# Hybrid decoder trunk on one Trainium2 core: the query latent and half of the key latent projected in three fp32r passes over split raw tokens

## The chip, the cores and the metric

The kernel runs on one core of one Trainium2 chip. The metric is the device time of one execution in microseconds (us). Before the change the median of three runs is 1300.8 us (1300.68 to 1301.29).

## What is computed

One layer of a decoder trunk on 272 tokens (16 learned meta tokens and 256 real ones) of width 1024: a Mamba-2 branch and a latent-attention branch side by side, then a mixture of 32 experts.

```python
hn = rms_norm(h, norm_mix[i])
u = hn @ w_in[i]
z, xbc, dt_raw, q_a, kv_a, gate_logits = jnp.split(u, IN_SPLITS, axis=-1)
y_ssd = ssd_branch(z, xbc, dt_raw, ...) @ w_ssd_out[i]
y_mla = mla_branch(q_a, kv_a, ...) @ w_o[i]      # begins with rms_norm(q_a), rms_norm(c_kv)
h = h + (g_ssd * y_ssd + g_mla * y_mla) @ w_out[i]
h = h + moe_ffn(rms_norm(h, norm_ffn[i]), ...)
```

The change touches two slices of the product `hn @ w_in`: `q_a` (384 columns, the query latent) and the block of 320 columns that the kernel calls `dkv` (32 of `dt_raw`, 256 of the key latent, 32 of its rotary part). Both latents are normed over their own columns afterwards.

## The kernel before

Everything runs in one program with one instruction stream for each engine, in an order written out by hand, with semaphores between the streams. Each engine takes its instructions in that order. ACT is ScalarE, DVE is VectorE, PE is TensorE, SP issues the DMAs.

**The front.** SP issues at the start, in this order: the transposed tokens in two halves (`hnT`), between and behind them the `dkv` weights in two halves, then the tokens in rows (`xtok`, four DMAs), the `qa` weights (1.5 MB, inside the loop over `SLABS`), the small vectors `vec`, and further weight slabs. DVE multiplies `hnT` by the gains of the norm, but not yet by the norm itself (L1072). PE multiplies this raw `hnT` by `dkv` and then by `qa` in plain float32 (the loops at L1622 to L1637 and L1647 to L1654). The token norms `rsx` come later, out of `xtok` (squares on ACT L657 and DVE L1076, then twelve tiny DVE steps in `rstd`, L1041 to L1064), and are multiplied in when ACT reads the banks (L679 to L688, L697 to L699). `spread_norms` on PE, behind the first `qa` matmul, broadcasts the norms over the partitions; DVE then makes `hnN`, the normed tokens (L1083), and ACT and DVE split it into a rounded part `hn_hi` (fp32r, L666) and the rest `hn_lo` (L1087).

**The feature units.** All other columns of `w_in` are made by `split_mm`: for each 128 columns the weights are split as well, `hi_of(p)` on ACT (L673) and `lo_of(p)` on DVE (L1100), into one of three buffers `split[p % 3]`, and PE makes three fp32r passes, hi·hi, hi·lo and lo·hi, over 8 blocks k. The first eight units, `cv` 0 to 7, feed a causal convolution. For unit c ACT reads the bank twice (`conv_in`, L707 and L712), DVE does three steps (`conv_of`, L1137 and L1138), ACT the tanh (`tanh_of`, L719), DVE the last product (`silu_of`, L1146). `conv_in(c)` waits, from c = 2 on, for `conv_of(c - 2)`, and PE's unit u waits until the bank of unit u - 2 has been read. The order on ACT in this stretch is

```python
for c in range(4):
    conv_in(c)
    hi_of(c + 3)
    if c:
        tanh_of(c - 1)
```

and on DVE

```python
for c in range(4):
    if c < 3:
        lo_of(c + 3)
    conv_of(c)
    if c:
        silu_of(c - 1)
```

Ahead of that loop DVE has `lo_of(0)` and `lo_of(1)`, the norm of the key latent (`rstd(rsk, ...)`), the rotary steps of `ckk` (L1108 to L1120), `lo_of(2)`, and the norm of the query latent (`rstd(rsq, ...)`, behind `proj_read` 5, ACT's read of the last `qa` bank). Behind the front come attention, the scan, the output projections (to about 384 us), and then the 32 experts, whose weights (about 400 MB) stream in as buffers come free.

## Time and profile before

| | |
|---|---|
| median of three runs | 1300.8 us (1300.68 to 1301.29) |
| the profiled execution's own time | 1301.11 us |
| its span in the profile | 1299.1 us |
| PE busy in the span | 1271.6 us (98%) |
| DVE busy | 461.1 us (35%) |
| ACT busy | 348.6 us (27%) |
| DMA | 467.24 MB, 360 GB/s in the mean |

One execution of the program is taken by the profiler. Times are from the start of the span. Some 2 us of the device time lie around the span (1301.11 less 1299.1). "Busy" is the time in which at least one instruction of the engine ran; the ends of matmuls are modelled. The share of an engine over the whole span says little about a stretch: DVE's 35% is an average over a first part in which it is nearly always busy and an expert part in which it idles.

### The profile page before, as it was taken

How to read it: one execution, taken by the hardware profiler on the slowest of the kernel's cores; microseconds unless marked ns; L12 is line 12 of the kernel's file. 1: busy time of each engine (PE TensorE's matmuls, PEld its weight loads, DVE VectorE, ACT ScalarE, POOL GpSimd, SP SyncE). 2: the span in 40 equal slices, each digit the busy share in tenths (PEclk: the TensorE clock that was granted, in tenths of full speed). 3: DMA queues.
4: the chain of work that ended last, by engine and by line, in shares of the span. 5: the costliest groups of instructions: out<-in, count | busy, mean ns of one | idle time of the engine just before them, and what ended most of it. 6: DMA issues, size and time to landing. Idle time of an engine off the chain costs nothing.

```text
span 1299.1 us, 17685 instructions
## 1 busy us (share of the span) xinstructions
PE 1271.6 (98%) x7139; PEld 646.0 (50%) x7139; DVE 461.1 (35%) x1072; ACT 348.6 (27%) x671; POOL 28.7 (2%) x46
## 2 busy tenths in 40 slices
PE   9999999999999999999999999999999999999997
PEld 7889999999973333333333233333333333323332
DVE  5978889887652112111121111112111112111112
ACT  4667788654441011110110110011110011010102
POOL 1000000022010000000000000000000000000000
PEclk9999999999999999999999999999999999999999
DMA  8332255457889999999999999999999999999996
GB/s 309 128 142 120 97 230 221 170 195 287 318 315 426 420 408 427 429 429 428 430 433 430 430 427 431 431 435 430 431 430 427 431 434 432 430 431 433 424 427 284
DMA packets 32180, 467.24 MB, mean 360 GB/s; under 512 B 4112, under 2 KB 4144, under 8 KB 8704
## 3 DMA queue, kind: packets, MB, share of 16 engines
q1 hardware_dynamic: 31840, 466.00, 85.8%
q8 instruction: 36, 0.59, 0.2%
q10 hardware_dynamic: 288, 0.52, 0.1%
q14 instruction: 16, 0.13, 0.0%
HBM read 465.43 MB, written 1.08 MB: 359 GB/s over the span
## 4 chain that ended last, share of the span: by engine, by line
PE 46%; DMA 23%; DVE 0%; SPq 0%; issue 0%; ACT 0%; DVEq 0%
PE bank L1593 44%; DMA ring<-wts_dram 16%; DMA work<-wts_dram 7%; PE bank L1994 1%; PE bank L2000 1%; PE bank L2024 1%; SPq L433 0%; SPq L567 0%; DVE work L1587 0%; DVE work L1553 0%; ACT work L1004 0%; DVE work L1497 0%; DVE work L1569 0%; DVEq L107 0%; DVE work L1499 0%
## 5 line engine op out<-in xcount | busy, mean ns | idle before, releaser
L1593 PE MATMUL bank<-ring,work 128*64 128x512 f32 (+2 forms) x2168 | 490.0, 586 | 13.1 <-DMA ring<-wts_dram 12.8
L1593 PE MATMUL bank<-work 128*64 128x512 f32 (+8 forms) x2184 | 430.3, 550 | 6.3 <-DMA work<-wts_dram 4.3
L1593 PEld LDWEIGHTS bank<-ring,work 128*64 128x64 f32 (+1 forms) x2168 | 156.4, 138 | 297.3 <-issue 263.9
L1593 PEld LDWEIGHTS bank<-work 128*64 128x64 f32 (+3 forms) x2184 | 148.5, 143 | 258.9 <-issue 239.1
L1593 PE MATMUL bank<-hn_hi,split 128*128 128x256 f32 (+1 forms) x896 | 172.2, 287 | 0.3 <-ACT work L712 0.2
L1520 DVE COPY work<-bank 128x256 f32<-128x256 f32 x30 | 12.7, 425 | 447.3 <-PE bank L2024 447.3
L1593 PEld LDWEIGHTS bank<-hn_hi,split 128*128 128x128 f32 x896 | 141.3, 188 | 1.0 <-ACT work L712 0.4
L1593 PE MATMUL bank<-hn_lo,split 128*128 128x256 f32 (+1 forms) x448 | 127.1, 284 | 0.0
L1100 DVE TENSOR_TENSOR split<-ring,split 128x1024 fp32r<-128x1024 f32 x88 | 109.7, 1248 | 23.1 <-ACT split L673 22.7
L1497 DVE TENSOR_SCALAR work<-bank 128x512 f32<-128x512 f32 x32 | 22.2, 692 | 262.5 <-PE bank L1593 262.5
L931 ACT ACTIVATE work<-bank 128x512 f32<-128x512 f32 x31 | 18.5, 598 | 325.6 <-PE bank L1593 325.6
L673 ACT ACTIVATE split<-ring 128x1024 fp32r<-128x1024 f32 x88 | 92.5, 1055 | 23.5 <-PE bank L1593 23.4
L1593 PEld LDWEIGHTS bank<-hn_lo,split 128*128 128x128 f32 x448 | 84.4, 188 | 0.1
L952 ACT ACTIVATE work<-bank 128x512 f32<-128x512 f32 x30 | 17.9, 598 | 190.1 <-PE bank L1593 190.1
L946 ACT ACTIVATE work<-bank 128x512 f32<-128x512 f32 x32 | 19.1, 598 | 155.0 <-PE bank L2000 155.0
L935 ACT ACTIVATE work<-bank 128x512 f32<-128x512 f32 x31 | 18.5, 598 | 105.8 <-PE bank L1994 105.8
L1593 PE MATMUL bank<-y_hi,split 128*128 128x256 f32 x256 | 46.2, 283 | 0.0
L1593 PEld LDWEIGHTS bank<-y_hi,split 128*128 128x128 f32 x256 | 40.0, 192 | 0.0
L1593 PE MATMUL bank<-y_lo,split 128*128 128x256 f32 x128 | 36.2, 283 | 0.0
L1593 PE MATMUL bank<-attn_hi,split 128*128 128x256 f32 (+1 forms) x144 | 28.2, 290 | 0.0
L2000 PEld LDWEIGHTS bank<-shifted,work 128*128 128x128 f32 x128 | 13.4, 140 | 26.0 <-issue 26.0
L832 ACT ACTIVATE work<-ring,small 128x256 f32<-128x256 f32 x64 | 24.4, 453 | 5.7 <-PE bank L1593 5.2
(302 smaller groups left out, 939.6 us busy)
## 6 DMA issues: line engine op xcount, KB each, us to landing
ring<-wts_dram SPq DMA_DIRECT2D x83, 2048.0 KB, 19.1
ring<-wts_dram SPq DMA_DIRECT2D x20, 4096.0 KB, 30.3
work<-wts_dram SPq DMA_DIRECT2D x20, 4096.0 KB, 29.3
ring<-slabs_dram SPq DMA_DIRECT2D x23, 2048.0 KB, 8.6
work<-wts_dram SPq DMA_DIRECT2D x23, 2048.0 KB, 14.4
...
```

Source lines behind the costliest of these rows:

```text
L673: a.activation(split[p % NSPLIT][:, 0], piece(p), ACT.Copy).then_inc(hi_ready, 1)
L832: last = a.activation(decay[c % 2][:, j, at:at + SEQ - lo], spread[:, c % 3, j, lo:SEQ], ACT.Relu, scale=-1.0, bias=As[:, col:col + 1])
L931: a.activation(xg[:, :], bank[7][:, :], ACT.Copy).then_inc(xg_ready, 1)
L935: a.activation(xgT[:, :, :].rearrange("p j t -> p (j t)"), bank[7][:, :], ACT.Copy).then_inc(xgT_ready, 1)
L946: a.activation(actT[:, :, :].rearrange("p j t -> p (j t)"), bank[7][:, :], ACT.Copy, scale=0.5).then_inc(actT_ready, 1)
L952: a.activation(ob[:, :], bank[6][:, :], ACT.Copy).then_inc(ob_ready, 1)
L1100: d.tensor_tensor(split[p % NSPLIT][:, 1], piece(p), split[p % NSPLIT][:, 0], ALU.subtract).then_inc(lo_ready, 1)
L1497: d.tensor_scalar(glu[:, :], bank[4][:, :], LIMIT, None, ALU.min).then_inc(glu_ready, 1)
L1593: return pe.matmul(o, lhsT, rhs, start=start, stop=stop)
L1994: last = pe.transpose(bank[7][:, j * P:(j + 1) * P], xg[:, j * P:(j + 1) * P], ident[:, :])
L2000: last = pe.transpose(bank[7][:, j * P:(j + 1) * P], act[:, j * P:(j + 1) * P], ident[:, :])
L2024: last = pe.transpose(bank[to][:, b * P:(b + 1) * P], hotw[:, b, :, :].rearrange("p i s -> p (i s)"), ident[:, :])
```

## The change

The `qa` product and blocks k = 4 to 7 of the `dkv` product, for the two blocks of 128 tokens, are no longer made in float32. The raw tokens, the `qa` weights and the second half of the `dkv` weights are each split into an fp32r part and the rest: ACT makes `raw_hi`, `dkv_w_hi` and `qa_w_hi`, DVE `raw_lo`, `dkv_w_lo` and `qa_w_lo`, and PE takes three fp32r passes over them. The last 16 tokens (`tail_latents`) stay in float32 and go ahead of the second half of the others. The `qa` weights are loaded in two halves, the first ahead of `xtok`, the second and `vec` behind it. The norms of both latents are made in one chain (`rsqrt` over five columns) behind `proj_read` 5. `lo_of(2)` comes ahead of that chain and `lo_of(3)` behind it; in the loop over c, `lo_of(4)` and `lo_of(5)` stand ahead of `conv_of(0)` and `conv_of(1)`. The `vec` scalings go behind `lo_of(1)`, and `hi_of(2)` on ACT goes between the two reads of the `qa` banks. New buffers overlay memory that is free at that time. The semaphores `hn_hi_ready` and `hn_lo_ready` become `front_hi_ready` and `front_lo_ready`, which count the new splits too. Left out below: the overlays and views, the names of the semaphores, and the two places of the loop over `SLABS` from which `qa` and `vec` are taken.

```diff
--- before.py
+++ after.py
...
@@ -398,15 +406,19 @@
 
         @block.sync
         def _(sp):
-            half_T, half_dkv = KD // 2 * L, KD // 2 * DKV
+            half_T, half_dkv, half_qa = KD // 2 * L, KD // 2 * DKV, KD // 2 * QL
+            qa_dram = slabs[:, OFF[SLAB["qa"]]:OFF[SLAB["qa"]] + 2 * half_qa]
             sp.dma_start(w(3072 - KD, KD + half_T), xt[:, 0:KD + half_T]).then_inc(xT_in[0], 16)
             sp.dma_start(slab("dkv")[:, 0:half_dkv], slabs[:, 0:half_dkv]).then_inc(dkv_half_in, 16)
             sp.dma_start(w(3072 + half_T, half_T), xt[:, KD + half_T:KD + 2 * half_T]).then_inc(xT_in[1], 16)
             sp.dma_start(slab("dkv")[:, half_dkv:2 * half_dkv], slabs[:, half_dkv:2 * half_dkv]).then_inc(slab_in[0], 16)
+            sp.dma_start(slab("qa")[:, 0:half_qa], qa_dram[:, 0:half_qa]).then_inc(qa_half_in, 16)
             sp.dma_start(xtok[NMETA:P, 0, :], x[0:P - NMETA, :]).then_inc(x_in[0], 16)
             sp.dma_start(xtok[0:NMETA, 0, :], meta).then_inc(x_in[0], 16)
             sp.dma_start(xtok[:, 1, :], x[P - NMETA:2 * P - NMETA, :]).then_inc(x_in[1], 16)
             sp.dma_start(xtok[0:TAIL, 2, :], x[2 * P - NMETA:SEQ, :]).then_inc(x_in[1], 16)
+            sp.dma_start(slab("qa")[:, half_qa:2 * half_qa], qa_dram[:, half_qa:2 * half_qa]).then_inc(slab_in[1], 16)
+            sp.dma_start(vec[:, :], vecs).then_inc(vec_in, 16)
 
             def pair_of(e, h):
                 return wts[bass.ds((e * E_UNITS + 2 * h) * P, 2 * P), :].rearrange("(p i) c -> p i c", i=2)
...
@@ -651,6 +661,21 @@
         def _(a):
             a.wait_ge(consts_ready, 2)
             a.activation(spare, small[:, 15:16], ACT.Square)
+            qa_w = slab("qa").rearrange("p (k n) -> p k n", k=KD)
+
+            def qa_hi_of(h):
+                ks = slice(h * (KD // 2), (h + 1) * (KD // 2))
+                a.activation(qa_w_hi[:, ks, :], qa_w[:, ks, :], ACT.Copy).then_inc(front_hi_ready, 1)
+
+            for h in range(2):
+                ks = slice(h * (KD // 2), (h + 1) * (KD // 2))
+                a.wait_ge(hnT_ready, h + 2)
+                a.activation(raw_hi[:, ks, :], hnT[:, ks, :], ACT.Copy).then_inc(front_hi_ready, 1)
+            a.wait_ge(*arrived("dkv"))
+            a.activation(dkv_w_hi, slab("dkv").rearrange("p (k n) -> p k n", k=KD)[:, KD // 2:KD, :],
+                         ACT.Copy).then_inc(front_hi_ready, 1)
+            a.wait_ge(qa_half_in, 16)
+            qa_hi_of(0)
             for b in (0, 2):
                 n = BLOCKS[b][1]
                 a.wait_ge(x_in[b // 2], 32)
...
@@ -663,7 +688,7 @@
 
             def hn_hi_of(i):
                 a.wait_ge(hnN_ready, i + 1)
-                a.activation(hn_hi[:, 4 * i:4 * i + 4, :], hnN[:, 4 * i:4 * i + 4, :], ACT.Copy).then_inc(hn_hi_ready, 1)
+                a.activation(hn_hi[:, 4 * i:4 * i + 4, :], hnN[:, 4 * i:4 * i + 4, :], ACT.Copy).then_inc(front_hi_ready, 1)
 
             def hi_of(p):
 
@@ -672,6 +697,8 @@
                     a.wait_ge(*PIECES[p - NSPLIT][2])
                 a.activation(split[p % NSPLIT][:, 0], piece(p), ACT.Copy).then_inc(hi_ready, 1)
 
+            a.wait_ge(*arrived("qa"))
+            qa_hi_of(1)
             a.wait_ge(rsx_ready, 1)
             for b in range(2):
                 a.wait_ge(proj_done, b + 1)
@@ -688,10 +715,12 @@
             a.activation(mid[0:TAIL, 2, :], tail_mid, ACT.Copy, scale=rsx[0:TAIL, 2:3]).then_inc(proj_read, 1)
             for j in range(2):
                 hn_hi_of(j)
-            for p in range(NSPLIT):
+            for p in range(2):
                 hi_of(p)
             a.wait_ge(rsxq_ready, 1)
             for b in range(2):
+                if b:
+                    hi_of(2)
                 a.wait_ge(proj_done, b + 4)
                 ps = bank[3 + b]
                 a.activation(junk2[:, 768 + b * QL:768 + (b + 1) * QL], ps[:, 0:QL], ACT.Square,
...
@@ -1071,22 +1100,43 @@
                 ks = slice(h * (KD // 2), (h + 1) * (KD // 2))
                 d.tensor_tensor(hnT[:, ks, :], hnT[:, ks, :], norm_mix[:, ks].unsqueeze(2).to_broadcast([P, KD // 2, L]),
                                 ALU.mult).then_inc(hnT_ready, 1)
+            qa_w = slab("qa").rearrange("p (k n) -> p k n", k=KD)
+
+            def front_lo_of(n, lo, whole, hi, h):
+                ks = slice(h * (KD // 2), (h + 1) * (KD // 2))
+                d.wait_ge(front_hi_ready, n)
+                d.tensor_tensor(lo[:, ks, :], whole[:, ks, :], hi[:, ks, :], ALU.subtract).then_inc(front_lo_ready, 1)
+
+            d.wait_ge(hnT_ready, 3)
+            front_lo_of(1, raw_lo, hnT, raw_hi, 0)
+            front_lo_of(2, raw_lo, hnT, raw_hi, 1)
+            d.wait_ge(front_hi_ready, 3)
+            d.tensor_tensor(dkv_w_lo, slab("dkv").rearrange("p (k n) -> p k n", k=KD)[:, KD // 2:KD, :], dkv_w_hi,
+                            ALU.subtract).then_inc(front_lo_ready, 1)
+            front_lo_of(4, qa_w_lo, qa_w, qa_w_hi, 0)
             d.wait_ge(consts_ready, 2)
             d.wait_ge(x_in[1], 32)
             link(d.tensor_tensor_reduce(out=junk[:, 1, :], in0=xtok[:, 1, :], in1=xtok[:, 1, :], scale=1.0, scalar=0.0,
                                         op0=ALU.mult, op1=ALU.add, accum_out=ssx[:, 1:2]))
             d.wait_ge(x_squared, 2)
             rstd(rsx, ssx, D, EPS, rsx_ready)
+            front_lo_of(5, qa_w_lo, qa_w, qa_w_hi, 1)
             d.wait_ge(rsx_spread, 1)
             d.tensor_copy(rsxq[:, :], bank[7][:, 0:2]).then_inc(rsxq_ready, 1)
             for i in range(2):
                 d.tensor_tensor(hnN[:, 4 * i:4 * i + 4, :], hnT[:, 4 * i:4 * i + 4, :],
                                 bank[6][:, 0:L].unsqueeze(1).to_broadcast([P, 4, L]), ALU.mult).then_inc(hnN_ready, 1)
             for i in range(2):
-                d.wait_ge(hn_hi_ready, i + 1)
-                d.tensor_tensor(hn_lo[:, 4 * i:4 * i + 4, :], hnN[:, 4 * i:4 * i + 4, :], hn_hi[:, 4 * i:4 * i + 4, :],
-                                ALU.subtract).then_inc(hn_lo_ready, 1)
-
+                front_lo_of(6 + i, hn_lo, hnN, hn_hi, i)
+
+            def lo_of(p):
+
+                d.wait_ge(hi_ready, p + 1)
+                d.tensor_tensor(split[p % NSPLIT][:, 1], piece(p), split[p % NSPLIT][:, 0], ALU.subtract).then_inc(lo_ready, 1)
+
+
+            for p in range(2):
+                lo_of(p)
             d.wait_ge(vec_in, 16)
             w_router = v("w_router").rearrange("p (k e) -> p k e", k=KD)
             d.tensor_tensor(w_router, w_router, v("norm_ffn").unsqueeze(2).to_broadcast([P, KD, E]), ALU.mult).then_inc(vec_scaled, 1)
...
@@ -1094,16 +1144,14 @@
             d.tensor_scalar(v("conv_b"), v("conv_b"), 0.5, None, ALU.mult).then_inc(vec_scaled, 1)
             link(d.tensor_scalar(v("ssd_norm"), v("ssd_norm"), 0.5, None, ALU.mult))
 
-            def lo_of(p):
-
-                d.wait_ge(hi_ready, p + 1)
-                d.tensor_tensor(split[p % NSPLIT][:, 1], piece(p), split[p % NSPLIT][:, 0], ALU.subtract).then_inc(lo_ready, 1)
-
-
-            for p in range(2):
-                lo_of(p)
-            d.wait_ge(proj_read, 3)
-            rstd(rsk, ssk, KVL, MLA_EPS)
+            lo_of(2)
+            d.wait_ge(proj_read, 5)
+            d.tensor_scalar(ssk, ssk, 1.0 / KVL, MLA_EPS, ALU.mult, ALU.add)
+            link(d.tensor_scalar(ssq, ssq, 1.0 / QL, MLA_EPS, ALU.mult, ALU.add))
+            rsqrt(sm(11, 5), sm(3, 5), nrt)
+            for b in range(2):
+                d.tensor_scalar(qa[:, b, :], qa[:, b, :], rsq[:, b:b + 1], None, ALU.mult)
+            lo_of(3)
             for b in range(NB):
                 d.tensor_scalar(ckk[:, b, 0:KVL], mid[:, b, HEADS_S:HEADS_S + KVL], rsk[:, b:b + 1], None, ALU.mult)
             d.memset(ckk[:, :, KVL:KVL + ROPE], 0.0)
@@ -1117,17 +1165,12 @@
             link(d.tensor_tensor(kr[:, 3], k1, sinv, ALU.mult))
             for at in (KVL + ROPE, KVL + 2 * ROPE):
                 d.tensor_tensor(ckk[:, :, at:at + 16], kr[:, 0], kr[:, 1], ALU.subtract)
-                d.tensor_tensor(ckk[:, :, at + 16:at + ROPE], kr[:, 2], kr[:, 3], ALU.add)
+                last = d.tensor_tensor(ckk[:, :, at + 16:at + ROPE], kr[:, 2], kr[:, 3], ALU.add)
+            last.then_inc(latent_ready, 1)
 
             dt3 = dtv.rearrange("p (b h) -> p b h", b=NB)
             link(d.tensor_tensor(dt3, mid[:, :, 0:HEADS_S], v("dt_bias").unsqueeze(1).to_broadcast([P, NB, HEADS_S]), ALU.add))
             d.scalar_tensor_tensor(dta[:, :], dtv[:, :], -1.0, dtv[:, :], ALU.mult, ALU.max).then_inc(dt_abs, 1)
-            lo_of(2)
-            d.wait_ge(proj_read, 5)
-            rstd(rsq, ssq, QL, MLA_EPS)
-            for b in range(2):
-                last = d.tensor_scalar(qa[:, b, :], qa[:, b, :], rsq[:, b:b + 1], None, ALU.mult)
-            last.then_inc(latent_ready, 1)
 
             def conv_of(c):
 
...
@@ -1148,8 +1191,8 @@
 
             d.wait_ge(consts_ready, 4)
             for c in range(4):
-                if c < 3:
-                    lo_of(c + 3)
+                if c < 2:
+                    lo_of(c + 4)
                 conv_of(c)
                 if c:
                     silu_of(c - 1)
...
@@ -1619,23 +1662,31 @@
             pe.wait_ge(hnT_ready, 1)
             fill(12)
             wsl = slab("dkv").rearrange("p (k n) -> p k n", k=KD)
-            for h in range(2):
-                pe.wait_ge(hnT_ready, h + 2)
-                if h:
-                    pe.wait_ge(*arrived("dkv"))
-                else:
-                    pe.wait_ge(dkv_half_in, 16)
-                for b, (t0, n) in enumerate(BLOCKS):
-                    for k in range(KD // 2 * h, KD // 2 * (h + 1)):
-                        if n == P:
-                            last = mm(bank[b][:, 0:DKV], hnT[:, k, t0:t0 + n], wsl[:, k, :], k == 0, k == KD - 1)
-                        else:
-                            for j in range(2):
-                                cols = slice(j * (DKV // 2), (j + 1) * (DKV // 2))
-                                last = mm(bank[b][32 * j:32 * j + n, 0:DKV // 2], hnT[:, k, t0:t0 + n], wsl[:, k, cols],
-                                          k == 0, k == KD - 1)
-                    if h:
-                        last.then_inc(proj_done, 1)
+            def tail_latents(h):
+                t0, n = BLOCKS[2]
+                for k in range(KD // 2 * h, KD // 2 * (h + 1)):
+                    for j in range(2):
+                        cols = slice(j * (DKV // 2), (j + 1) * (DKV // 2))
+                        mm(bank[2][32 * j:32 * j + n, 0:DKV // 2], hnT[:, k, t0:t0 + n], wsl[:, k, cols], k == 0, k == KD - 1)
+
+            pe.wait_ge(hnT_ready, 2)
+            pe.wait_ge(dkv_half_in, 16)
+            for b in range(2):
+                for k in range(KD // 2):
+                    mm(bank[b][:, 0:DKV], hnT[:, k, b * P:(b + 1) * P], wsl[:, k, :], k == 0, False)
+            tail_latents(0)
+            pe.wait_ge(hnT_ready, 3)
+            pe.wait_ge(*arrived("dkv"))
+            tail_latents(1)
+            pe.wait_ge(front_lo_ready, 3)
+            for b in range(2):
+                for i in range(KD // 2):
+                    hi, lo = (raw[:, KD // 2 + i, b * P:(b + 1) * P] for raw in (raw_hi, raw_lo))
+                    mm(bank[b][:, 0:DKV], hi, dkv_w_hi[:, i, :], False, False)
+                    mm(bank[b][:, 0:DKV], lo, dkv_w_hi[:, i, :], False, False)
+                    last = mm(bank[b][:, 0:DKV], hi, dkv_w_lo[:, i, :], False, i == KD // 2 - 1)
+                last.then_inc(proj_done, b + 1)
+
             def spread_norms():
                 pe.wait_ge(consts_ready, 1)
                 pe.wait_ge(rsx_ready, 1)
...
@@ -1644,13 +1695,17 @@
                 mm(bank[7][:, 0:2], shifted[:, P:2 * P], rsx[:, 0:2], True, False)
                 mm(bank[7][:, 0:2], shifted[0:NMETA, 0:P], rsx[0:NMETA, 1:3], False, True).then_inc(rsx_spread, 1)
 
-            wsl = take("qa").rearrange("p (k n) -> p k n", k=KD)
             for b in (1, 2):
                 ps = bank[2 + b]
+                rows = slice(NMETA + (b - 1) * P, NMETA + b * P)
                 for k in range(KD):
                     if b == 1 and k == 1:
                         spread_norms()
-                    last = mm(ps[:, 0:QL], hnT[:, k, NMETA + (b - 1) * P:NMETA + b * P], wsl[:, k, :], k == 0, k == KD - 1)
+                    if b == 1:
+                        pe.wait_ge(front_lo_ready, 4 + k // (KD // 2))
+                    mm(ps[:, 0:QL], raw_hi[:, k, rows], qa_w_hi[:, k, :], k == 0, False)
+                    mm(ps[:, 0:QL], raw_hi[:, k, rows], qa_w_lo[:, k, :], False, False)
+                    last = mm(ps[:, 0:QL], raw_lo[:, k, rows], qa_w_hi[:, k, :], False, k == KD - 1)
                 last.then_inc(proj_done, 1)
 
             def feature_unit(kind, i, p, t0):
```

## Rows read from the trace of the kernel before

**Rows 1.** The page: busy time of the engines; DMA rate in 40 slices

```profile
PE 1271.6 (98%) x7139; PEld 646.0 (50%) x7139; DVE 461.1 (35%) x1072; ACT 348.6 (27%) x671; POOL 28.7 (2%) x46
...
GB/s 309 128 142 120 97 230 221 170 195 287 318 315 426 420 408 427 429 429 428 430 433 430 430 427 431 431 435 430 431 430 427 431 434 432 430 431 433 424 427 284
```

**Rows 2.** Stretches: window, length, busy PE, PEld, DVE, ACT, POOL, clock, DMA, GB/s

```profile
30.00:62.00 32.00, 31.81 (x237) 29.31 (x236) 30.33 (x81) 21.13 (x42) 0.43 (x1) 1.00 0.39 141
...
340.00:384.00 44.00, 44.00 (x282) 39.72 (x281) 24.39 (x40) 20.16 (x31) 5.63 (x4) 1.00 0.73 276
```

**Rows 3.** Timeline (start, duration, engine, line, operation, count), PE in the front

```profile
18.70 0.93 PE L1593 MATMUL bank<-shifted,small 128*128 128x128 f32 x6
...
20.18 9.94 PE L1593 MATMUL bank<-ring,work 128*128 128x384 f32 x30
29.66 0.58 PE L1593 MATMUL bank<-hn_hi,split 128*128 128x272 f32 x1
```

**Rows 4.** Timeline, PE in the query units: single fp32r passes of 384 columns

```profile
72.99 0.33 PE L1593 MATMUL bank<-uq_lo,split 128*128 128x384 f32 x1
...
73.16 0.34 PE L1593 MATMUL bank<-uq_hi,split 128*128 128x384 f32 x1
```

**Rows 5.** Timeline, DVE and ACT in the front; the last row is the page's DMA list

```profile
13.54 1.23 DVE L1076 CUSTOM_DVE_ANT_0 work<-work 128x1024 f32<-128x1024 f32 x1 [4.87 <-DMA work<-x_dram]
...
17.18 0.47 ACT L679 ACTIVATE work<-bank,small 128x256 f32<-128x256 f32 x1 [2.62 <-DVE small L1056]
...
20.29 0.16 DVE L1081 COPY small<-bank 128x2 f32<-128x2 f32 x1 [3.14 <-PE bank L1593]
...
21.67 2.31 ACT L666 ACTIVATE hn_hi<-work 128x1088 fp32r<-128x1088 f32 x2 [1.08 <-DVE work L1083]
22.82 2.49 DVE L1087 TENSOR_TENSOR hn_lo<-work,hn_hi 128x1088 fp32r<-128x1088 f32 x2
...
ring<-slabs_dram SPq DMA_DIRECT2D x1, 1536.0 KB, 12.2
```

**Rows 6.** Timeline of DVE from the front to the convolutions

```profile
26.09 2.36 DVE L1100 TENSOR_TENSOR split<-ring,split 128x1024 fp32r<-128x1024 f32 x2
...
28.37 0.16 DVE L1064 TENSOR_SCALAR small<-small 128x3 f32<-128x3 f32 x1
...
30.75 0.88 DVE L1108 TENSOR_SCALAR work<-work,small 128x256 f32<-128x256 f32 x3
...
38.53 1.04 DVE L1137 SCALAR_TENSOR_TENSOR work<-work,vec 128x272 f32<-128x272 f32 x2
...
47.05 0.50 DVE L1138 SCALAR_TENSOR_TENSOR work<-work,vec 128x272 f32<-128x272 f32 x1
```

**Rows 7.** Timeline of ACT: reads of the banks, splits of weights, tanh

```profile
30.73 0.57 ACT L699 ACTIVATE work<-bank,small 128x384 f32<-128x384 f32 x1
...
33.94 1.06 ACT L673 ACTIVATE split<-ring 128x1024 fp32r<-128x1024 f32 x1
...
40.14 0.44 ACT L719 ACTIVATE work<-work 128x272 f32<-128x272 f32 x1 [2.12 <-DVE work L1138]
...
41.22 1.06 ACT L673 ACTIVATE split<-ring 128x1024 fp32r<-128x1024 f32 x1
...
47.59 0.43 ACT L719 ACTIVATE work<-work 128x272 f32<-128x272 f32 x1 [1.41 <-DVE work L1138]
```

**Rows 8.** Timeline: where PE and its weight loads wait for ACT

```profile
53.25 0.39 PE L1593 MATMUL bank<-hn_hi,split 128*128 128x272 f32 x1 [0.19 <-ACT work L712]
...
62.84 1.59 PEld L1593 LDWEIGHTS bank<-ring,work 128*128 128x128 f32 x6 [0.75 <-ACT work L751]
```

**Rows 9.** Stretch and timeline in the experts, where the clock fell

```profile
1140.00:1142.00 2.00, 1.75 (x4) 0.53 (x6) 0.00 (x0) 0.00 (x0) 0.00 (x0) 0.53 1.06 459
1142.00:1144.00 2.00, 2.00 (x8) 0.61 (x6) 0.00 (x0) 0.00 (x0) 0.00 (x0) 0.62 0.95 410
...
1140.25 5.26 PE L1593 MATMUL bank<-work 128*64 128x512 f32 x16 [1.78 <-DMA work<-wts_dram]
```

More of the change, by code:

```diff
@@ L124, in meta_ssd_mla_moe @@
                 end = at + n
+        for name, at, n in [("dkv_w_lo", IN_WORK + 20224, KD // 2 * DKV), ("dkv_w_hi", IN_WORK, KD // 2 * DKV), ("qa_w_lo", SLOT, KD * QL), ("raw_hi", IN_WORK + 9600, KD * L), ("raw_lo", IN_WORK + 21504, KD * L),
+                            ("qa_w_hi", IN_WORK + 25736, KD * QL)]:
+            with ExitStack() as lent:
+                lent.enter_context(nc.sbuf_tensor(f"before_{name}", [P, at], F32))
+                overlays[name] = lent.enter_context(nc.sbuf_tensor(name, [P, n], F32R))
         ring = sb("ring", NSLOT * SLOT)
@@ L152, in meta_ssd_mla_moe @@
         hn_lo = overlays["hn_lo"][:, :].rearrange("p (k t) -> p k t", k=KD)
+        raw_hi, raw_lo, qa_w_hi, qa_w_lo = (overlays[n][:, :].rearrange("p (k t) -> p k t", k=KD)
+                                            for n in ("raw_hi", "raw_lo", "qa_w_hi", "qa_w_lo"))
+        dkv_w_hi, dkv_w_lo = (overlays[n][:, :].rearrange("p (k t) -> p k t", k=KD // 2) for n in ("dkv_w_hi", "dkv_w_lo"))
         spread = ring[:, 3 * SLOT + 2464:3 * SLOT + 2464 + 3 * 2 * SEQ].rearrange("p (i j t) -> p i j t", i=3, j=2)
@@ L269, in meta_ssd_mla_moe @@
         ssh, rsh, cmax = sm(796, 2), sm(798, 2), sm(800, 1)
-        nrt = sm(801, 3)
+        nrt = sm(801, 5)
         rsxq = sm(804, 2)
@@ L443, in _ @@
             for i, (name, n) in enumerate(SLABS):
-                if name == "dkv":
+                if name in ("dkv", "qa"):
                     continue
@@ L458, in _ @@
                         spread_rows(c)
[L459 to L461 removed]
+                if name == "g0":
                     load_w1(1, 1, True)
@@ L1660, in feature_unit @@
                          True).then_inc(proj_done, 1)
-            pe.wait_ge(hn_lo_ready, 2)
+            pe.wait_ge(front_lo_ready, 7)
             for c in range(5):
```

9 lines of the change are left out of this document (3 added, 6 removed).

## The prediction, written before the changed kernel was run

> **What bounds the kernel now.** I read the page first, then the busy time by stretches, then the timeline of one engine after the other up to 63 us. The page says that PE is busy for 98% of the span [rows 1], and by stretches it is busy for 31.81 of 32 us from 30 to 62 and for all of 340 to 384 [rows 2]; the stretches between look the same. So up to 384 us what PE loses or gains stays. Behind that the experts' weights stream at some 430 GB/s [rows 1], each load issued when PE has freed its buffer, so the stream starts later or earlier with PE, and I pass a shift on one to one.
>
> The second reading is the one that decides here. From 30 to 62 us DVE is busy for 30.33 of 32 us [rows 2], and its timeline has no wait from 26.09 to some 60 us [rows 6]. PE itself waits twice in this stretch, both times for ACT: at 53.25 for the read of a unit's bank (L712) and near 62.84 for a read at L751 [rows 8]. ACT in turn was waiting for DVE: its tanh instructions at 40.14 and 47.59 sat idle 2.12 and 1.41 us until `conv_of` was done [rows 7]. The reader is to see that in this stretch PE is tied to the chain DVE, ACT, PE, with DVE as its continuous part. A change that shortens PE's work gains there only what it also takes from DVE's chain.
>
> The profiled execution took 1301.11 us, 0.3 more than the median of 1300.8. I work out a shift against its rows and add it to the median.
>
> **Part 1: PE's work.** A float32 matmul of 384 columns stands as two records. From 20.18 to 29.66 there are 15 of them, 0.63 us each [rows 3]. An fp32r pass of 384 columns starts 0.17 us after the one ahead (72.99 to 73.16) [rows 4], so three take 0.52. Sixteen matmuls save 16 x 0.11 = 1.8 us. For 320 columns I scale both by 320/384: 0.53 against 0.43, eight matmuls, 0.8 us. The 16-token part only moves. PE's work falls by 2.6 us.
>
> **Part 2: when the token norms come.** The first half of `qa` (786 KB) now goes ahead of the four `xtok` DMAs. Before, DVE began its square at 13.54, released by the last of these, and the whole `qa`, issued at 4.74, landed 12.2 us later, at 16.9 [rows 5]. So 1.5 MB took about 3.5 us behind `xtok`, and half of it delays `xtok` by 1.8. The norm `rsx`, which released ACT at 17.18 [rows 5], comes at 19.0. The bounds of this delay are 0 (if it hid in a gap of the queue) and 2.5 us; I take 1.8, since the DMAs landed in the order of their issue.
>
> The Trainium skill, "DMA: Bandwidth & Descriptors", section "Queues, rings and completion order", says that each DMA engine consumes the descriptors of a queue in ring order. By that rule the whole 1.8 us falls on `xtok`, without it at most a part; the sum below would be +1.3 or, with no delay, +0.7.
>
> The new splits themselves fit in time that was idle. By the pitch of the old ones, 1.24 us on DVE for 1088 columns and 1.15 on ACT [rows 5], ACT makes both halves of `raw_hi` from 5.8 and 8.7 us, `dkv_w_hi` (1280 columns) by 11.1 and the first half of `qa_w_hi` (1536 columns, 1.6 us) by 12.8; DVE ends `dkv_w_lo` at 12.7 and the first `qa_w_lo` at 14.6. Before, DVE idled 4.87 us ahead of 13.54 and 3.14 ahead of 20.29, and ACT 2.62 ahead of 17.18 [rows 5]: that is the cover. PE has done the 16 tokens and the first half by 13.4 and needs `dkv_w_lo` only then; its three passes end at 17.0, its first `qa` step at 17.6. There it meets `spread_norms`, which waits for `rsx`: PE idles 1.4 us, to 19.1. The step itself takes 1.5 (18.70 to 20.18) [rows 3], then 15 x 0.52 = 7.8: PE ends `qa` at 28.4 instead of 29.66. Of 2.6 us saved 1.2 are left.
>
> DVE has the second `qa_w_lo` (1.7 us) between `rsx` and the copy of the spread norms. That copy moves from 20.29 to 20.8. But ACT reads the three `dkv` banks only from 19.0 on, 1.8 later, and `hn_hi` stands behind them in its queue: it begins at 22.5 instead of 21.67 [rows 5], and `hn_lo`, whose second half needs the second `hn_hi`, ends at 26.05 instead of 25.25. DVE's chain starts 0.8 us late.
>
> **Part 3: DVE up to the first convolution.** Before, `conv_of(0)` began at 38.53 [rows 6], 13.3 us behind the end of `hn_lo`. The merged norms take out eleven small instructions: twelve took 28.37 to 30.75, 0.2 each [rows 6], so 2.2 us go. One `lo_of` more (1.14 each, 26.09 to 28.37 for two [rows 6]) stands ahead of `conv_of(0)`: five instead of four. `proj_read` 5 is no wait: ACT's last read of `qa` ended at 31.30 [rows 7], 1.6 behind 29.66, now at about 30.1, and DVE arrives at 30.4. `lo_of(3)` waits a little for `hi_of(3)`, which comes behind `conv_in(0)`: 33.94 - 29.66 behind the start of unit 0 [rows 3, 7] plus 1.06 gives 33.75, and DVE is there at 33.6. With 0.2 for this, DVE begins `conv_of(0)` at 26.05 + 13.3 - 2.2 + 1.1 + 0.2 = 38.5: as before. The late start is paid back.
>
> **Part 4: a new wait.** Now `lo_of(5)` stands ahead of `conv_of(1)`, and it needs `hi_of(5)`. On ACT `hi_of(5)` stands behind `tanh_of(0)` and `conv_in(2)`, and both wait for `conv_of(0)`. So DVE, done with `conv_of(0)` at 40.1, must sit until ACT has run tanh, two reads and the split: from 40.14 to 41.22 + 1.06 = 42.28 in the old timeline, 2.14 us [rows 7], and 0.1 for the hand-over. Before, `lo_of(4)` and `conv_of(1)` filled this time and the split was waiting when DVE came. The wait is 2.2 us; its bounds are 2.0 (nothing of it can run earlier, the order is fixed) and 2.4. Queued behind it on DVE are all convolutions up to 60 us. Against it stands one `lo_of` that has gone from the loop (-1.14). Up to `conv_of(3)`, whose last step ended at 47.55 [rows 6], the sum is 0.0 + 2.2 - 1.1 = +1.1, and 0.1 to 0.2 more because `silu_of(3)` now waits for ACT: +1.3. ACT's tanh at 47.59 [rows 7] goes to 48.9 and everything behind it on ACT and DVE, a continuous chain, goes with it.
>
> **Part 5: PE behind it.** PE starts unit 0 1.2 us early. At unit 4 it waits some 0.6 for `conv_in(2)`, at unit 6 for `lo_of(6)` (its end goes from 49.6 to 50.9), at unit 7 for the L712 read that held it at 53.25 already, and at the third query unit for L751 [rows 8]. The last two are moved by the full +1.3, so that is PE's shift. From there it is busy to 384, and the shift stays.
>
> **Sum: +1.3 us, 1300.8 + 1.3 = 1302.1 us.** The forecast's own range: with no delay of `xtok` the start is late by only 0.25 (ACT still has the second `qa_w_hi` until 18.5), which gives +0.7; with a delay of 2.5 us +2.0; the wait of part 4 adds 0.2 either way. 1301.3 to 1303.0.
>
> **The rivals.**
>
> *A, the DVE chain has slack and PE's own saving shows.* Then unit 0 starts 1.2 us early, 0.6 go at unit 4, and 0.6 are left: 1300.2 us. For it speaks that PE's two old waits are short [rows 8]; against it that DVE is busy for 30.33 of 32 us [rows 2]. Chance 0.13.
>
> *B, all of PE's saving arrives*, because `xtok` is not delayed and the splits wait for nobody: -2.6 to -2.8 us, 1298.1. It needs part 2 and part 4 both wrong. Chance 0.04.
>
> *C, slower: the clock falls in PE's new idle time at 17.6 us.* The granted clock was 0.53 in 1140 to 1142 and 0.62 in 1142 to 1144, behind an idle time of 1.78 us [rows 9]: most of both at the lower of its two levels, 1.2 of 2.4 GHz, 1.9 + 1.5 = 3.4 us of low clock. If the same comes here, half of these 3.4 us are lost in the `qa` product: it ends 1.7 us later, at 30.1, ACT's read at 31.8, and DVE, which now does have to wait for `proj_read` 5, starts its norms 1.4 late. Sum +2.7 to +2.8, 1303.6 us. It decides once the idle time is like that 1.78 us; I work out 1.4, and `xtok` half a microsecond later than I think would bring it there. Chance 0.12.
>
> The Trainium skill, "TensorE: Matmul & The Clock Gate", section "What's actually happening", says that the throttled clock is the default and that activity releases it, which speaks against any new idle time on PE. By that rule alone, if 1.4 us of idleness is enough, the sum would be rival C's +2.7, else +1.3. Rows 9 agree in kind: one idle time and a fall behind it; whether a shorter one does it they don't show.
>
> *D, the change doesn't do what it says:* a split turned into more passes or a wait that I overlooked, another +1 us or more. Chance 0.03.
>
> **How the numbers follow.** Forecast 0.68, A 0.13, B 0.04, C 0.12, D 0.03. The range reaches down to A's 1300.2 and up to C's 1303.7; outside lie B and D and the edges of A and C, under 2 in 10. A measurement of this kernel can tell about 0.2%, 2.6 us, from no change: faster means below 1298.2 (B and the lower edge of A: 0.05), slower above 1303.4 (most of C and all of D, 0.13), and the rest, 0.82, is no difference.
>
> **What would show it.** In the changed profile: DVE's square of `xtok` at 15.4; PE idle from 17.6 to 19.1; the last `qa` pass near 28.4; `hn_lo` ending at 26.0; a DVE idle time of 2.2 us ahead of the `lo_of` at 42.4, released by ACT's split; ACT's tanh of unit 3 at 48.9; PE's query unit behind L751 at 64.1 instead of 62.84. If the idle time at 40 us is there but that query unit starts earlier than 62.84, the chain was not the bound and A holds; if the clock row at 18 to 22 us is below 1.00, C does. The prediction is wrong from its root if PE's stretches from 63 to 384 don't shift as a whole.

## The result, and the profile after

The changed kernel takes 1305.75 us in the median of seven runs (1304.98 to 1306.33), the kernel before 1300.8. The ratio is 1.0035 with an interval of [1.0026, 1.0045]: slower by 3.4 to 5.9 us. The forecast was 1302.1, its range ended at 1303.7. Two single runs far outside all others, one of e3 (3291 us) and one of the kernel before (4032 us), are left out of the reading below.

The time is lost in the first 66 us. One reference point is used throughout: the scatter copy of the third expert, which stood at 449.97 us in the kernel before. Below is that row in the timeline of DVE, after:

```profile
453.40 0.42 DVE L1563 COPY work<-bank 128x256 f32<-128x256 f32 x1 [16.39 <-PE bank L2079]
```

The shift there is 3.43 us. At the third query unit it is 3.49 already: PE's weight load behind ACT's read, 62.84 before [rows 8], stands now at

```profile
66.33 1.59 PEld L1636 LDWEIGHTS bank<-ring,work 128*128 128x128 f32 x6 [0.67 <-ACT work L780]
```

The profiled execution's span is 1303.0 us, 3.9 more than before, so some 0.5 us more comes behind the third expert. That part differs from trace to trace, from -0.5 (e2) to +0.8 us (e3), and says nothing in a single one. What happened ahead of 66 us is in three views of the changed kernel. First the timeline of PE (start, duration, line, operation, count, idle time ahead of it and its releaser):

```profile
17.33 0.34 PE L1636 MATMUL bank<-qa_w_hi,raw_lo 128*128 128x384 f32 x1
19.94 1.00 PE L1636 MATMUL bank<-shifted,small 128*128 128x128 f32 x6 [2.27 <-DVE small L1085]
20.87 0.69 PE L1636 MATMUL bank<-small,shifted 128*128 128x2 f32 x4
...
22.21 0.52 PE L1636 MATMUL bank<-qa_w_hi,raw_lo 128*128 128x384 f32 x1
22.53 0.52 PE L1636 MATMUL bank<-qa_w_hi,raw_hi 128*128 128x384 f32 x1
...
25.24 0.34 PE L1636 MATMUL bank<-qa_w_hi,raw_hi 128*128 128x384 f32 x1
25.42 0.34 PE L1636 MATMUL bank<-qa_w_lo,raw_hi 128*128 128x384 f32 x1
```

Before, PE was busy for all of 17 to 20 us:

```profile
17.00:20.00 3.00, 3.00 (x27) 2.15 (x23) 0.15 (x1) 2.77 (x10) 0.00 (x0) 1.00 1.02 429
```

Now it is through with its first `qa` step at 17.7 and waits 2.27 us for the token norms. Behind that a pass of 384 columns takes 0.32 us (22.21 to 22.53), and from 25 us on 0.18 (25.24 to 25.42). The busy time by stretches (after) says why; the column behind POOL is the granted clock:

```profile
20.00:21.60 1.60, 1.60 (x11) 1.42 (x12) 1.46 (x2) 1.60 (x7) 0.00 (x0) 1.00 1.01 430
21.60:25.00 3.40, 3.40 (x11) 3.40 (x12) 3.29 (x4) 3.36 (x8) 0.00 (x0) 0.50 1.00 424
25.00:30.00 5.00, 5.00 (x30) 5.00 (x29) 4.93 (x9) 4.28 (x7) 0.00 (x0) 1.00 0.39 167
```

PE has the lower of its two levels, 1.2 GHz, for 3.4 us in the middle of the `qa` product. The third view is the timeline of DVE:

```profile
16.18 1.23 DVE L1119 CUSTOM_DVE_ANT_0 work<-work 128x1024 f32<-128x1024 f32 x1 [0.71 <-DMA work<-x_dram]
...
24.26 2.49 DVE L1108 TENSOR_TENSOR hn_lo<-work,hn_hi 128x1088 fp32r<-128x1088 f32 x2
...
32.43 0.17 DVE L1149 TENSOR_SCALAR small<-small 128x3 f32<-128x3 f32 x1 [1.40 <-ACT work L728]
...
44.66 1.23 DVE L1135 TENSOR_TENSOR split<-ring,split 128x1024 fp32r<-128x1024 f32 x1 [2.20 <-ACT split L698]
```

The square of `xtok` comes at 16.18 instead of 13.54 [rows 5]; `hn_lo` ends at 26.75 instead of 25.3; DVE then waits 1.40 us for ACT's read of the last `qa` bank, and 2.20 us for `hi_of(5)` ahead of `lo_of(5)`. DVE had neither wait before. Of the shift of 3.43 us, 1.44 stand at the end of `hn_lo` and 1.40 in the wait for `proj_read` 5; the other 0.6 is what the new order leaves on DVE, its waits for the splits less the instructions that it saves.

### The profile page after: what moved, and what is told of

Same layout as the page of the kernel before. It is cut to its first block, busy times and chain, and to the rows that moved or that the text cites. A ratio compares the mean times of both kernels' runs of the same rounds, so it can differ in the third digit from the quotient of the medians.

```text
span 1303.0 us, 17734 instructions
## 1 busy us (share of the span) xinstructions
PE 1271.6 (98%) x7163; PEld 650.2 (50%) x7163; DVE 466.7 (36%) x1066; ACT 354.1 (27%) x676; POOL 28.6 (2%) x46
## 4 chain that ended last, share of the span: by engine, by line
PE 46%; DMA 23%; DVE 0%; SPq 0%; ACT 0%; issue 0%; DVEq 0%
PE bank L1636 44%; DMA ring<-wts_dram 16%; DMA work<-wts_dram 7%; PE bank L2049 1%; PE bank L2055 1%; PE bank L2079 1%; SPq L445 0%; SPq L577 0%; DVE work L1630 0%; DVE work L1596 0%; ACT work L1033 0%; DVE work L1612 0%; DVE work L1540 0%; DVEq L107 0%; DVE work L1542 0%
## 5 line engine op out<-in xcount | busy, mean ns | idle before, releaser
L1636 PE MATMUL bank<-ring,work 128*64 128x512 f32 (+3 forms) x2120 | 474.4, 588 | 12.6 <-DMA ring<-wts_dram 11.9
L1636 PEld LDWEIGHTS bank<-ring,work 128*64 128x64 f32 (+2 forms) x2120 | 147.4, 137 | 291.0 <-issue 261.2
```

The source lines that it names most:

```text
L1636: return pe.matmul(o, lhsT, rhs, start=start, stop=stop)
```

## The experiments

All times of several runs are medians. "Before" ran beside each group: 1301.03 us for the first four, 1300.90 for the next four, 1301.01 for the last four. The third column is the difference; the shift is that of the third expert's copy in the profiled run, against 449.97. A shift is good to some 0.6 us: in the trace of e4, which is the kernel before up to 77 us, the row behind L751 stands at 62.26 instead of 62.84.

| kernel | us | against before | shift of the profiled run |
|---|---|---|---|
| changed kernel | 1305.75 | +4.95 | +3.43 |
| e1: `lo_of(5)` late | 1303.72 | +2.7 | +1.42 |
| e2: PE's wait filled | 1303.27 | +2.2 | +1.29 |
| e3: both | 1301.67 | +0.6 | +0.05 |
| e4: before, delayed | 1304.53 | +3.5 | +2.96 |
| e5: `xtok` first | 1302.73 | +1.8 | +0.12 |
| e6: `xtok` first, `lo_of(5)` late | 1299.92 | -1.0 | -1.48 |
| e7: before, `lo_of(5)` early | 1303.37 | +2.5 | +2.00 |
| e8: before, `qa` half first | 1302.56 | +1.7 | +1.63 |
| e9: changed kernel, one run | 1302.31 | +1.3 | +1.37 |
| e10: changed kernel, one run | 1306.07 | +5.1 | +4.75 |
| e11: before, one chain of norms | 1301.54 | +0.5 | +0.12 |
| e12: e6 with a short fill | 1299.87 | -1.1 | -1.86 |

**e1: the place of `lo_of(5)`.** On the changed kernel:

```diff
-                if c < 2:
-                    lo_of(c + 4)
+                if c in (0, 2):
+                    lo_of(4 + c // 2)
                 conv_of(c)
```

> The changed kernel with lo_of(5) back behind conv_of(1), ahead of conv_of(2). Theory 1 (the order on DVE costs a wait that the whole chain carries): the DVE idle time of 2.20 us at 42.5 is gone, the second half of it is not replaced because hi_of(5) is ready when DVE comes, so PE's third query unit starts 1.8 us earlier than in the changed kernel (64.5 instead of 66.3) and the time falls by 1.8 us, to 1303.9. Theory 2 (DVE has slack behind 42 us and the loss lies in the front alone, in late norms and a lower clock): within 0.3 us of the changed kernel, 1305.7.

Measured: 1303.72 us (1300.89 to 1304.97), ratio to before 1.0019 [1.0010, 1.0028], 2.0 us less than the changed kernel. DVE's waits by line and releaser (total, times, longest), from 26 to 66 us:

```profile
DVE small L1149 <- ACT work L728: 1.4, 1, 1.4
DVE split L1135 <- ACT split L698: 0.8, 2, 0.5
```

In the changed kernel the second row read 2.7, 2, 2.2. The wait of 2.20 us is gone; 0.36 of it is left. The shift falls by 2.01 us between two traces that both have 3.4 us of low clock, so the time follows the wait: DVE has no slack there. The runs spread over 4 us, and here the granted clock goes with them: the mean of a run is 0.996 in the four fastest and 0.994 or 0.995 in the seven others.

**e2: PE's idle time filled.** On the changed kernel:

```diff
                     if b == 1 and k == 1:
+                        fill(10)
                         spread_norms()
```

> The changed kernel with ten small float32 matmuls on PE (2.1 us of work nobody needs) in its idle time ahead of spread_norms. Theory 1 (that idle time costs a fall of the clock, and with it DVE's wait of 1.40 us for proj_read 5): granted clock 1.00 from 21.6 to 25.0 us instead of 0.50, the last qa pass 1.7 us earlier, no DVE wait at 32.4, time down by 1.4 us, to 1304.3. Theory 2 (the fall is hidden by the DVE chain, since DVE would have waited anyway or catches up): same time as the changed kernel, 1305.7. Theory 3 (the clock falls for another reason than the idle time): the clock row stays at 0.50.

Measured: 1303.27 us (1301.83 to 1303.73), ratio 1.0017 [1.0009, 1.0026], 2.5 us less than the changed kernel, with more instructions. The stretch:

```profile
21.60:25.00 3.40, 3.40 (x22) 3.40 (x21) 3.34 (x4) 3.39 (x6) 0.00 (x0) 1.00 0.99 419
```

The clock stays at its upper level, 22 matmuls are recorded in the stretch instead of 11, and DVE's wait for `proj_read` 5 is gone. One trace would not prove it, since e9 below has no fall either. But the trace of e3 has none, and the mean granted clock is 0.996 or more in all runs of e2 and e3, where it is 0.993 to 0.995 in six of the changed kernel's seven. So the pause brings the fall, and the fall costs at least the 1.4 us of that wait. Between the two profiled runs the shift falls by 2.14: the 1.4, and 0.73 because `xtok` landed that much earlier (15.45 against 16.18). What the median gains beyond 1.4 fits with runs in which the clock stays low for longer (e10).

With the clock up in every run, the median is still 2.2 us above the kernel before, not the 1.3 of the forecast. So the clock is not all of the miss, though the filling itself may have a small part: in this trace DVE waits 0.20 us for `spread_norms` behind it.

**e3: both edits.**

> Both edits, lo_of(5) behind conv_of(1) and ten matmuls in PE's idle time. If the two losses lie one behind the other on the DVE chain they add: 1.8 + 1.4 = 3.2 us down, 1302.5. If one hides the other, 1303.9 or more. What stays above the kernel before is then the late token norms.

Measured: 1301.67 us, ratio 1.0004 [0.9995, 1.0013]: 4.1 us less than the changed kernel, where the two alone gave 2.0 and 2.5. They add, nearly in full, as two losses one behind the other on the same chain do. (The 3.2 expected was too small by the part of e2.)

**e4: a delay and nothing else.** On the kernel before, 78 us into it:

```diff
+            pe.wait_ge(q_roped, 1)
+            fill(16)
             q_pair(0)
```

> The kernel before with sixteen small float32 matmuls (3.4 us at full clock) on PE at 78 us, ahead of the first transposes of the queries: nothing but a delay, of the size that the change brings by 100 us. Theory A (a shift ahead of the experts arrives one to one): 1300.8 + 3.4 = 1304.2. Theory B (the experts add to a shift, by other falls of the clock or another meeting with the weight stream): 1305.2 to 1305.8, as the changed kernel.

Measured: 1304.53 us (1304.11 to 1305.19), ratio 1.0028 [1.0018, 1.0038], +3.5. In the trace the filling takes 3.57 us (77.48 to 81.05), and the shift goes from -0.58 at 62 us to +2.96 at the third expert, by 3.54. A shift ahead of the experts reaches the end one to one, so the bulk of the 4.95 us of the changed kernel must arise in the front, in runs other than its first profiled one (e10).

**e5: `xtok` ahead of `qa`.** On the changed kernel, with the steps on ACT, DVE and PE put in the order in which the data now come:

```diff
-            sp.dma_start(slab("qa")[:, 0:half_qa], ...).then_inc(qa_half_in, 16)
             sp.dma_start(xtok[NMETA:P, 0, :], ...)
...
+            sp.dma_start(slab("qa")[:, 0:half_qa], ...).then_inc(qa_half_in, 16)
             sp.dma_start(slab("qa")[:, half_qa:2 * half_qa], ...).then_inc(slab_in[1], 16)
...
-            a.wait_ge(qa_half_in, 16)
-            qa_hi_of(0)
             for b in (0, 2):
                 ...                          # ACT's squares of xtok
+            a.wait_ge(qa_half_in, 16)
+            qa_hi_of(0)
...
-            front_lo_of(4, qa_w_lo, qa_w, qa_w_hi, 0)
             d.wait_ge(consts_ready, 2)
...
             rstd(rsx, ssx, D, EPS, rsx_ready)
+            front_lo_of(4, qa_w_lo, qa_w, qa_w_hi, 0)
             front_lo_of(5, qa_w_lo, qa_w, qa_w_hi, 1)
...
+            spread_norms()
             for b in (1, 2):
...
-                    if b == 1 and k == 1:
-                        spread_norms()
```

> The changed kernel with the four xtok DMAs ahead of both halves of qa again, and the steps that depend on it in that order: ACT squares xtok ahead of the first qa_w_hi, DVE makes both halves of qa_w_lo behind the token norms, PE has spread_norms ahead of the first qa pass. lo_of(5) stays where the change put it. Theory 1 (late norms and the clock fall they bring cost 1.4 + 1.4, the lo_of order 1.8 to 2.0): token norms at 17.2 us, no idle time of PE above 0.5 us and clock 1.00 throughout, hn_lo ends at 25.5, no DVE wait for proj_read 5, the 2.2 us DVE wait at 40 us is still there: 1301.03 + 0.5 = 1301.5. Theory 2 (the splits themselves lengthen the front whatever the order): 1303.5 or more.

Measured: 1302.73 us (1301.00 to 1303.82), ratio 1.0010 [1.0001, 1.0019]. The profiled run is as theory 1 says: DVE's square at 13.58, PE busy for all of 17 to 20 us at clock 1.00, no wait for `proj_read` 5, and the wait of 2.20 us for `hi_of(5)`. Its shift is 0.1, and its own time, 1301.34, is near the 1301.5 expected. But the median lies 1.2 us above the expectation, not far from theory 2's 1303.5, though the mean clock of the runs does not differ (0.996 to 0.997 in all but one). That part isn't explained (below).

**e6: `xtok` first and `lo_of(5)` late,** e5 with the edit of e1.

> As the run before, and lo_of(5) behind conv_of(1). Theory 1: both causes are gone, and what is left is the gain of the merged norms on the DVE chain (11 instructions of 0.2 us) less some 0.8 us of waits for ACT's splits: 1.4 us faster than the kernel before, 1299.6. Theory 2 (the splits lengthen the front): no faster than 1301.

Measured: 1299.92 us (1298.82 to 1301.82), ratio 0.9992 [0.9983, 1.0001]. 5.8 us faster than the changed kernel; against the kernel before 1.0 us, with an interval that just includes none. So the splits, the three passes and the merged norms are no loss in themselves; whether they are a gain stays just inside the noise, here and in e12. DVE's waits from 14 to 64 us:

```profile
DVE split L1135 <- ACT split L698: 0.4, 1, 0.4
DVE work L1189 <- ACT work L748: 0.2, 1, 0.2
```

**e7: the place of `lo_of(5)` alone,** on the kernel before:

```diff
-                if c < 3:
-                    lo_of(c + 3)
+                if c == 0:
+                    lo_of(3)
+                    lo_of(4)
+                elif c == 1:
+                    lo_of(5)
                 conv_of(c)
```

> The kernel before with one thing of the change: lo_of(4) ahead of conv_of(0) and lo_of(5) ahead of conv_of(1). Theory 1: DVE waits 2.2 us for hi_of(5) and the chain carries it all to PE: 1301.03 + 2.2 = 1303.2. Theory 2 (the DVE chain has slack): 1301.0 to 1301.6.

Measured: 1303.37 us (1302.32 to 1303.91), ratio 1.0017 [1.0008, 1.0026]: +2.5. The row that answers to the one at 44.66 above:

```profile
43.23 1.23 DVE L1100 TENSOR_TENSOR split<-ring,split 128x1024 fp32r<-128x1024 f32 x1 [2.20 <-ACT split L673]
```

The same wait to the hundredth, in a kernel with none of the other edits.

**e8: the order of the loads alone,** on the kernel before: `qa` in halves, the first ahead of `xtok`, the second and `vec` behind it.

```diff
...
+            sp.dma_start(slab("qa")[:, 0:half_qa], ...).then_inc(qa_half_in, 16)
             sp.dma_start(xtok[NMETA:P, 0, :], ...)
...
             sp.dma_start(xtok[0:TAIL, 2, :], ...)
+            sp.dma_start(slab("qa")[:, half_qa:2 * half_qa], ...).then_inc(slab_in[1], 16)
+            sp.dma_start(vec[:, :], vecs).then_inc(vec_in, 16)
...
+            pe.wait_ge(qa_half_in, 16)
             wsl = take("qa").rearrange("p (k n) -> p k n", k=KD)
```

> The kernel before with one thing of the change: qa in two halves, the first ahead of xtok, the second and vec behind it. Theory 1: token norms 2.3 us later (19.4), PE idle for some 0.8 us ahead of spread_norms, hn_lo 1.4 us later and the whole chain with it, clock 1.00 because the idle time is short: 1302.4. Theory 2 (the delay is hidden by PE's float32 work): 1301.0 to 1301.4. If the clock falls all the same: 1303.5 or more.

Measured: 1302.56 us (1301.34 to 1305.63), ratio 1.0011 [1.0002, 1.0021]: +1.7. The timeline of PE in e8:

```profile
19.42 1.00 PE L1595 MATMUL bank<-shifted,small 128*128 128x128 f32 x6 [0.85 <-DVE small L1058]
...
32.16 0.58 PE L1595 MATMUL bank<-hn_hi,split 128*128 128x272 f32 x1
```

and its busy time by stretches, with the granted clock behind POOL:

```profile
20.00:21.60 1.60, 1.60 (x8) 1.22 (x8) 0.52 (x2) 1.59 (x6) 0.00 (x0) 0.87 1.10 471
21.60:25.00 3.40, 3.40 (x7) 1.88 (x6) 3.29 (x4) 3.37 (x7) 0.00 (x0) 0.56 0.98 410
...
30.00:62.00 32.00, 32.00 (x238) 29.48 (x237) 30.14 (x84) 20.20 (x40) 0.43 (x1) 1.00 0.39 141
```

The total is near the 1302.4 of theory 1, but partly by luck. DVE's chain is late by less than expected: `hn_lo` ends 0.93 us later (26.24), not 1.4. And the clock fell here too, for 3.4 us by the first two rows, behind an idle time of only 0.85. DVE never waits for it: in the kernel before the norm of the key latent stands on DVE ahead of the wait for `proj_read` 5, so a late `qa` product was covered there. The merged chain took that cover away. But PE pays: its first feature unit starts at 32.16 instead of 29.66 [rows 3], and from 30 to 62 us it has no idle time left. So the shift of 1.63 is PE's own, some 0.7 more than DVE's chain would bring, and that is about what the fall costs here (an estimate from these rows).

**e9 and e10: the changed kernel, two more traces.**

> The changed kernel itself, a second trace. In its first trace the shift against the kernel before is 3.43 us at the third expert and 3.9 at the end, while its runs lie 4.95 above in the median. Theory A (the loss beyond 3.4 us arises in the front, where DMAs land at other times from run to run and nothing covers a late one any more): in a run near 1305.7 the shift at the third expert is itself 4.5 or more, with the token norms later than 19.8 us or the clock lower for longer. Theory B (it arises in the experts): that shift is 3.4 again and the rest comes behind 650 us.

> A third trace of the changed kernel, for the same two theories: A, shift at the third expert of 4.5 or more with a total near 1305.7; B, 3.4 there and the rest in the experts. If both traces come out near 1305.0 neither is told apart.

Measured: 1302.31 and 1306.07 us. First e9, busy time and granted clock of the stretch from 21.6 to 25 us:

```profile
21.60:25.00 3.40, 3.40 (x21) 3.40 (x20) 3.29 (x4) 3.40 (x6) 0.00 (x0) 1.00 0.94 400
```

and the reference row in its timeline of DVE:

```profile
451.34 0.42 DVE L1563 COPY work<-bank 128x256 f32<-128x256 f32 x1 [16.39 <-PE bank L2079]
```

Then e10, the stretches:

```profile
20.00:21.60 1.60, 1.60 (x9) 1.42 (x8) 1.32 (x1) 1.60 (x7) 0.00 (x0) 0.64 1.06 451
21.60:25.00 3.40, 3.40 (x11) 3.38 (x12) 2.92 (x4) 2.89 (x7) 0.00 (x0) 0.50 1.00 424
25.00:30.00 5.00, 5.00 (x24) 5.00 (x24) 4.96 (x8) 4.26 (x7) 0.00 (x0) 0.77 0.37 157
```

and the timeline of DVE, with the wait for `proj_read` 5 and the reference row:

```profile
33.74 0.17 DVE L1149 TENSOR_SCALAR small<-small 128x3 f32<-128x3 f32 x1 [1.92 <-ACT work L728]
...
454.72 0.42 DVE L1563 COPY work<-bank 128x256 f32<-128x256 f32 x1 [16.39 <-PE bank L2079]
```

The same program, three traces, three lengths of low clock: none in e9 (shift 1.37), 3.4 us in the first trace (3.43), and in e10 1.2 + 3.4 + 2.3 = 6.9 us by the three rows (4.75). Theory A holds: the shift of e10 stands at the third expert in full. PE idled about as long in all three, 2.01 us (e9), 2.27 and 2.20.

The length of a pause alone does not decide either. In the changed kernel PE idles a second time, at 53 us, longer than the 0.85 of e8, and the clock stays up. First the timeline row (after), then the stretch:

```profile
53.28 0.36 PE L1636 MATMUL bank<-hn_hi,split 128*128 128x272 f32 x1 [1.34 <-DVE split L1135]
...
50.00:54.00 4.00, 2.66 (x22) 2.47 (x21) 3.80 (x8) 2.89 (x7) 0.00 (x0) 1.00 0.01 2
```

The traces of e2, e5, e7, e9 and e10 have this pause too (1.34 or 1.35 us), also at clock 1.00. Behind the pause in the front stand the ten small products of `spread_norms`, behind this one full passes. Whether that is the difference no run separates.

**e11: one chain of norms alone,** on the kernel before, with `lo_of(5)` late. The moved `lo_of`, `hi_of` and `vec` steps are left out:

```diff
...
-            d.wait_ge(proj_read, 3)
-            rstd(rsk, ssk, KVL, MLA_EPS)
+            lo_of(2)
+            d.wait_ge(proj_read, 5)
+            d.tensor_scalar(ssk, ssk, 1.0 / KVL, MLA_EPS, ALU.mult, ALU.add)
+            link(d.tensor_scalar(ssq, ssq, 1.0 / QL, MLA_EPS, ALU.mult, ALU.add))
+            rsqrt(sm(11, 5), sm(3, 5), nrt)
...
```

> The kernel before with the chain of norms alone: both latent norms in one chain behind proj_read 5, lo_of(3) behind it, lo_of(4) ahead of conv_of(0), but lo_of(5) behind conv_of(1), so without the wait at 42 us; float32 passes and the order of loads as before. Theory 1 (eleven instructions, 2.2 us, go, but without PE's earlier end of qa DVE sits idle for 1.8 us ahead of proj_read 5 and some more for ACT's splits): 1301.0 to 1301.4. Theory 2 (the merged norms alone are what made the sixth experiment faster): 1299.9 or less.

Measured: 1301.54 us, ratio 1.0005 [0.9996, 1.0014]. DVE waits for `proj_read` 5, 1.23 us, and for three splits, 1.3 us in all:

```profile
30.95 0.17 DVE L1109 TENSOR_SCALAR small<-small 128x3 f32<-128x3 f32 x1 [1.23 <-ACT work L701]
```

The 2.2 us of the eleven instructions saved are eaten by waits. So the chain alone does not pay; with an earlier end of `qa` on PE, in e6, those waits are 0.4 us.

**e12: e6 with `fill(3)` ahead of `spread_norms()`.**

> The sixth experiment (xtok first, lo_of(5) late) with three small float32 matmuls ahead of spread_norms, in the half microsecond in which PE still waited for the token norms. If that idle time now and then costs a fall of the clock, the runs lie closer together and lower, 1299.4 in the median; if the spread of 3 us between runs has its cause in the landing of the DMAs, nothing changes: 1299.9.

Measured: 1299.87 us (1299.54 to 1301.97), ratio 0.9992 [0.9983, 1.0001]. The median is that of e6. The lowest six of eleven runs lie within 0.4 us, in e6 within 1.1; whether that is the filling or chance these runs don't show.

## Why the prediction was wrong

The step that failed is in part 2: a new pause of PE was held to leave the clock alone. It lowered it for 3.4 us in the first trace, and DVE, for which `proj_read` 5 was to be no wait, waited 1.40 us. A second term, the delay of `xtok`, was too small: 1.8 us against 2.64 in that trace, which put `hn_lo` 1.44 us late instead of 0.8. The two make up nearly all of the 2.1 us between the forecast shift of 1.3 and the 3.43 measured.

The rest of the path came as written. e9 is the forecast nearly to the number, 1302.31 against 1302.1, shift 1.37 against 1.3, but it is the only one of nine runs of this kernel below 1304.9. And with the clock up in every run (e2) the median is 1303.27, so even with a clock that stays up the forecast would have been some 1 us short.

- **Part 1, PE's work.** Right. Three passes of 384 columns took 0.53 us (0.176 each at the upper clock), three of 320 columns 0.44.
- **Part 2, the delay of `xtok`.** Too small. 1.8 us was taken and 2.5 named as the upper bound; the square came 2.64 us late in the first trace (16.18 against 13.54), 2.07 in e9, 2.50 in e10. The moment varies from run to run even with the old order, from 13.39 (e12) to 14.38 (e7). The mean of seven traces with the old order is 13.74, of seven with the new one 15.87: 2.1 us. The step took its price from the bytes behind `xtok`, at 0.43 MB/us. Ahead of it the loads of the kernel before ran slower, at 353 GB/s, by which 786 KB take 2.2 us (an estimate from this row of before):

```profile
4.00:13.50 9.50, 9.50 (x50) 7.08 (x49) 2.59 (x2) 1.24 (x3) 0.61 (x3) 1.00 1.04 353
```

- **Part 2, the idle time of PE.** Forecast at 1.4 us, measured 2.0 to 2.5, since the norms came later still. The forecast held that the clock would stay up, with 0.12 for the other case, on the ground that 1.4 is less than the 1.78 us of rows 9. One idle time that brought a fall says nothing on the shortest that does. Even 1.4 us would have been no safe ground: e8 shows a fall behind 0.85 us, e9 none behind 2.01. In this place it came in four of the five traces with such a pause.
- **Rival C's price.** Its mechanism came as written: `qa` late, ACT's read late, DVE waiting for `proj_read` 5. It was priced at 2.7 to 2.8 us with 3.4 us of low clock; it came to 3.43 with that, since the norms were 0.6 us later too, and to 4.75 with 6.9 us of low clock, a length for which the trace of before had no row.
- **Part 3, DVE up to the first convolution.** Right where the clock stayed up: in e9 `hn_lo` ends at 26.2 (26.05 forecast), and the wait for `lo_of(3)` was 0.42 for 0.2.
- **Part 4, the new wait.** Right: 2.20 us for 2.2, in every trace with that order. Undoing it gave 2.0 us (e1); doing it alone cost 2.5 (e7).
- **Part 5 and the one-to-one passage.** Right: e4. The shift at the query unit was that of the third expert within 0.1 in every trace but e4's, whose delay stands between the two. Rival A is excluded by e1 and e7, rival B by e9, where the clock stayed up and the shift was still +1.37.
- **The Trainium skill.** "TensorE: Matmul & The Clock Gate", section "What's actually happening", says that the throttled clock is the default and activity releases it. The traces agree: the granted clock fell behind the pause in the front in two traces of three and stayed up once PE was kept busy (e2). This rule was a better guide than the comparison with one row, though the pause at 53 us, without a fall, shows that it does not settle each case.

What stays open: the runs of e1, e5 and e6 spread over 3 to 4 us, those of the kernel before and of e7 over 1.5 to 2. In e1 the clock goes with it, in e5 and e6 it doesn't. One part is in the traces. Before, PE came to `spread_norms` at 18.70, 1.5 us behind norms that were ready at 17.18, and a late `xtok` was covered: its square ranges from 13.42 to 14.38 in four traces without the change's front (before, e4, e7, e11), and `hn_lo` ends at 24.7 to 25.3, no later for the later ones. With the change nothing covers it: `hn_lo` ends 10.6 us behind the square in the traces of the changed kernel, e1, e2, e3 and e9, and 11.9 behind it in e5, e6 and e12, to 0.02 us. So each late landing is passed on whole. But the landings seen lie within 1 us; that they make the 3 us of e5 is not shown, nor is why e2's median stands above the forecast.
